# Even mixer's feature norms: sums of all heads as rows of one tile, one pass of roots, spread by split-format products, squares shared between two engines

## The reference, cut to what matters

```
def rms_norm(x, g):
    xf = x.astype(jnp.float32)
    y = xf * lax.rsqrt(jnp.mean(jnp.square(xf), axis=-1, keepdims=True) + EPS)
    return (y * g.astype(jnp.float32)).astype(x.dtype)

    qn = rms_norm(q, q_norm).reshape(B, S, G, R, dk)
    ks_blk = to_blocks(rms_norm(k_sel, k_norm[1]))
    kw_pad = jnp.pad(rms_norm(k_win, k_norm[2]), pad)
    q = (rms_norm(c_q, cq_norm) @ w_uq).reshape(B, S, H, dn + dr)
    kv = (rms_norm(c_kv, ckv_norm) @ w_ukv).reshape(B, S, H, dn + dv)
```

## Time and profile before

| | before |
|---|---|
| median of three runs | 2292.04 us |
| lowest and highest run | 2291.61, 2302.24 us |
| the profiled execution's own time | 2293.38 us |
| its span, first to last instruction | 2291.6 us |
| PE, DVE, ACT, POOL busy | 93%, 56%, 43%, 8% of the span |
| mean granted TensorE clock | 0.970 of 2.4 GHz |

### The profile page before, as it was taken

One profiled execution on the slowest core, in us unless ns is written; L12 is line 12 of the kernel. 1 busy time (PEld: TensorE's weight loads), 2 busy tenths in 40 slices (PEclk: granted clock), 3 DMA queues, 4 the chain that ended last, 5 costly groups with the idle time before them and its releaser, 6 DMA issues. The chain is left out here.

```text
span 2291.6 us, 33139 instructions
## 1 busy us (share of the span) xinstructions
PE 2137.0 (93%) x12537; PEld 1652.5 (72%) x12537; DVE 1284.4 (56%) x1814; ACT 994.1 (43%) x1308; POOL 186.9 (8%) x182
## 2 busy tenths in 40 slices
PE   7987898999999999998999999998999789988998
PEld 5764434788888878888887888786577368777776
DVE  3367756353233234434666666888367754525888
ACT  2146636252123121121656665774243643414774
POOL 0010000000000000000311101011112300002011
PEclk9999989999999999998999999999999899988999
DMA  8007001153144135012878877995220000126996
GB/s 251 12 10 250 37 16 40 37 152 101 61 119 124 33 98 178 1 37 96 278 272 277 287 267 271 385 391 217 78 74 28 12 1 1 75 84 199 389 373 258
DMA packets 220721, 336.42 MB, mean 147 GB/s; under 512 B 50413, under 2 KB 135309, under 8 KB 220606
## 3 DMA queue, kind: packets, MB, share of 16 engines
q1 hardware_dynamic: 213470, 314.53, 40.6%
q0 software_dynamic: 7136, 20.34, 2.5%
HBM read 306.82 MB, written 26.95 MB: 146 GB/s over the span
## 5 line engine op out<-in xcount | busy, mean ns | idle before, releaser
L1550 DVE TENSOR_TENSOR moe_pass_wL<-moe_pass_w,moe_pass_wH 128x2048 fp32r<-128x2048 f32 (+1 forms) x144 | 303.4, 2112 | 113.2 <-ACT moe_pass_wH L1474 113.1
L1474 ACT ACTIVATE moe_pass_wH<-moe_pass_w 128x2048 fp32r<-128x2048 f32 (+1 forms) x144 | 254.7, 1772 | 130.4 <-PE PS L568 90.9
L1550 DVE TENSOR_TENSOR hm_pass_wL<-hm_pass_w,hm_pass_wH 128x2048 fp32r<-128x2048 f32 x60 | 135.7, 2287 | 36.3 <-ACT hm_pass_wH L1474 36.3
L566 PE MATMUL PS<-moe_pass_wL,moe_pass_xgH 128*128 128x512 f32 (+1 forms) x384 | 147.3, 384 | 6.9 <-DVE moe_pass_wL L1550 4.5
L568 PE MATMUL PS<-moe_pass_wH,moe_pass_xgH 128*128 128x512 f32 (+1 forms) x384 | 142.7, 372 | 0.0
L567 PE MATMUL PS<-moe_pass_wH,moe_pass_xgL 128*128 128x512 f32 (+1 forms) x384 | 142.6, 371 | 0.0
L566 PE MATMUL PS<-xnT_low,ffn_upH 128*128 128x512 f32 x352 | 140.2, 398 | 0.3 <-PE PS L568 0.3
L568 PE MATMUL PS<-ffn_xH,ffn_upH 128*128 128x512 f32 x352 | 138.3, 393 | 0.0
L567 PE MATMUL PS<-ffn_xH,ffn_up_low 128*128 128x512 f32 x352 | 137.6, 391 | 0.0
L73 PE MATMUL PS<-ones,ident 128*128 128x128 f32 x926 | 120.9, 293 | 13.4 <-PEq L42 11.1
L73 PEld LDWEIGHTS PS<-ones,ident 128*128 128x128 f32 x926 | 116.9, 207 | 18.3 <-issue 15.4
(11 more groups left out here) (843 smaller groups left out, 4946.1 us busy)
## 6 DMA issues: line engine op xcount, KB each, us to landing
moe_pass_w<-in_moe_w_down SPq DMA_DIRECT2D x40, 1024.0 KB, 6.9
moe_pass_w<-in_moe_w_gate SPq DMA_DIRECT2D x32, 1024.0 KB, 7.0
moe_pass_w<-in_moe_w_up SPq DMA_DIRECT2D x32, 1024.0 KB, 7.8
hm_pass_w<-in_exp_w_gate SPq DMA_DIRECT2D x40, 512.0 KB, 6.9
hm_pass_w<-in_exp_w_up SPq DMA_DIRECT2D x40, 512.0 KB, 6.9
hm_pass_w<-in_exp_w_down SPq DMA_DIRECT2D x40, 512.0 KB, 6.6
od_W<-in_od_w_in SPq DMA_DIRECT2D x12, 1024.0 KB, 11.2
moe_pass_w<-in_moe_w_gate SPq DMA_DIRECT2D x16, 768.0 KB, 6.9
```

The source lines that it names most:

```text
L566: nc.tensor.matmul(out, lh, rl, start=start, stop=False)
L1474: nc.scalar.activation(wH[:, i % S, 0:n], w[:, i % R, 0:n], ACT.Copy).then_inc(s["high"], 1)
L1550: nc.vector.tensor_tensor(wL[:, i % S, 0:n], w[:, i % R, 0:n], f32(wH[:, i % S, 0:n]), ALU.subtract) \
```

## The change

Six things are changed, all in or for `ev_hidden`:

- **Squares.** ACT squares the tiles 0, 2, 4, 6, 8 and POOL the tiles 1, 3, 5, 7, into nine buffers that are not reused.
- **Sums.** PE multiplies each square by its own 128x46 slice of a constant (`norm_sums`), accumulating all nine in one PSUM bank. Row r of 14 holds head r's mean square (rows 0 to 11 the heads, 12 cq, 13 ckv); rows 32 to 45 hold the same again.
- **Roots.** Ln, Exp and the Newton step are made once, over 46x512.
- **Split.** DVE rounds the 46 rows to fp32r into `both` (which POOL has zeroed), and then overwrites rows 32 to 45 by the low part.
- **Spread.** PE multiplies `both` by a constant of zeros and ones (`norm_spread`, rounded once by DVE at the stage's start, at the address of pcT) and so puts each head's root on the partitions of its head, one fp32r product per group, in four PSUM banks. DVE's final multiplication reads the root from PSUM.
- **Order.** PE makes the sums first, then hidden 0 and 1, roots 0 to 3, hidden 2, roots 4 to 7, hidden 3, and 12 instead of 40 `stay_busy` products. Two loads (212 KB and 524 KB) are added in the middle of `smalls`.

```
+    srcs = [src for grp in groups for src in grp["src"]]
+    high, low = slice(0, FSUMS), slice(LOW, FSUMS)
+    by_act = range(0, len(srcs), 2)
...
             nc.gpsimd.memset(ec[:, :], EPS).then_inc(s["eps"], 1)
+            nc.gpsimd.memset(f32(both[:, :]), 0.0).then_inc(s["eps"], 1)
+            for m, src in enumerate(srcs):
+                if m not in by_act:
+                    nc.gpsimd.tensor_tensor(sq[:, m], src, src, ALU.mult).then_inc(s["squared_p"], 1)
...
-            def sums(g):
-                if g >= NB:
-                    pe.wait_ge(s["normed"], first[g - NB + 1])
-                for i, src in enumerate(groups[g]["src"]):
-                    m = first[g] + i
-                    pe.wait_ge(s["squared"], m + 2)
-                    nc.tensor.matmul(PS[:, g % NB, :], groups[g]["ones"], sq[:, m % 4], start=i == 0,
-                                     stop=i == len(groups[g]["src"]) - 1).then_inc(s["summed"], 1)
+            def sums():
+                pe.wait_ge(loaded["small"], small)
+                for m in range(len(srcs)):
+                    if m in by_act:
+                        pe.wait_ge(s["squared_a"], m // 2 + 1)
+                    else:
+                        pe.wait_ge(s["squared_p"], m // 2 + 1)
+                    ins = nc.tensor.matmul(PS[high, 0, :], row_sum[:, m], sq[:, m], start=m == 0, stop=m == len(srcs) - 1)
+                ins.then_inc(s["summed"], 1)
...
+            def roots(g):
+                pe.wait_ge(s["rstd"], 1)
+                pe.wait_ge(s["spread_high"], 1)
+                if g >= 4:
+                    pe.wait_ge(s["normed"], done[g - 3])
+                nc.tensor.matmul(root_bank(g), row_spread[:, g], both[:, :], start=True, stop=True).then_inc(s["roots"], 1)
...
-            stay_busy(nc, C, 40, 4)
+            stay_busy(nc, C, 12, 4)
...
+            for m in by_act:
+                nc.scalar.activation(sq[:, m], srcs[m], ACT.Square).then_inc(s["squared_a"], 1)
+            act.wait_ge(s["eps"], 1)
+            act.wait_ge(s["summed"], 1)
+            nc.scalar.activation(rs[:, :], PS[high, 0, :], ACT.Ln, bias=ec[high, 0:1]).then_inc(s["logged"], 1)
+            act.wait_ge(s["logged"], 1)
+            nc.scalar.activation(rs[:, :], rs[:, :], ACT.Exp, scale=-0.5).then_inc(s["rooted"], 1)
...
+            nc.vector.tensor_copy(row_spread[:, :, :].rearrange("p a b -> p (a b)"), row_whole[:, :, :].rearrange("p a b -> p (a b)"))                 .then_inc(s["spread_high"], 1)
...
+            y, t = rs[:, :], tt[:, :]
+            dve.wait_ge(s["rooted"], 1)
+            step(nc.vector.scalar_tensor_tensor(out=t, in0=PS[high, 0, :], scalar=EPS, in1=y, op0=ALU.add, op1=ALU.mult))
+            step(nc.vector.scalar_tensor_tensor(out=t, in0=t, scalar=-0.5, in1=y, op0=ALU.mult, op1=ALU.mult))
+            step(nc.vector.scalar_tensor_tensor(out=y, in0=t, scalar=1.5, in1=y, op0=ALU.add, op1=ALU.mult))
+            dve.wait_ge(s["eps"], 2)
+            step(nc.vector.tensor_copy(both[high], y))
+            nc.vector.tensor_tensor(both[low], rs[low], f32(both[low]), ALU.subtract).then_inc(s["rstd"], 1)
+            for g, grp in enumerate(groups):
+                dve.wait_ge(s["roots"], g + 1)
+                for src, gain, dst in zip(grp["src"], grp["gain"], grp["dst"]):
+                    nc.vector.scalar_tensor_tensor(out=dst, in0=src, scalar=gain, in1=root_bank(g),
+                                                   op0=ALU.mult, op1=ALU.mult).then_inc(s["normed"], 1)
```

More of the change, by code:

```diff
@@ L1706 @@
 NH, HD = 8, 64
+LOW, FSUMS = 32, 46
 CMP_L, CMP_S = 32, 16
@@ L1757, in head_of_row, with norm_rows, norm_sums, norm_spread @@
     return pick
+def norm_rows():
+    rows = np.zeros((P, 9, 14), np.float32)
+    for p in range(P):
+        for m in range(6):
+            rows[p, m, 2 * m + p // HD] = 1.0
+    rows[:, 6:8, 12] = 1.0
+    rows[:, 8, 13] = 1.0
+    return rows
+def norm_sums():
+    count = np.array([HD] * 12 + [2 * P, P], np.float32)
+    out = np.zeros((P, 9, FSUMS), np.float32)
+    for a in (0, LOW):
+        out[:, :, a:a + 14] = norm_rows() / count
+    return out.reshape(P, 9 * FSUMS)
+def norm_spread():
+    out = np.zeros((P, 8, P), np.float32)
+    for a in (0, LOW):
+        out[a:a + 14] = norm_rows()[:, (0, 1, 2, 3, 4, 5, 6, 8)].transpose(2, 1, 0)
+    return out.reshape(P, 8 * P)
 def gains_by_row(q, k):
@@ L2035, in mixer_even, with norms_and_hidden, root_bank @@
         nc.all_engine_barrier(sem_only=True)
-def norms_and_hidden(nc, C, groups, kc, vc, X, pos, pair, w1, hid, hid4, gate, gq, gm, flip, flip32, loaded, small, load_table):
-    B, NB = 4, 4
-    G = len(groups)
-    batches = [range(a, min(a + B, G)) for a in range(0, G, B)]
-    with ExitStack() as mem, stage(nc, "ev_hidden", "ready spread X_taken squared summed logged rstd steps normed hid_made gelu sigmoid copied made") as (block, s):
-        sq = mem.enter_context(nc.sbuf_tensor("ev_hidden_sq", [P, 4, SEQ], F32))
-        rs = mem.enter_context(nc.sbuf_tensor("ev_hidden_rs", [P, 2 * B, SEQ], F32))
-        tt = mem.enter_context(nc.sbuf_tensor("ev_hidden_tt", [P, 2, SEQ], F32))
+def norms_and_hidden(nc, C, groups, kc, vc, X, pos, pair, w1, hid, hid4, gate, gq, gm, flip, flip32, loaded, small, load_table, row_sum, row_whole, row_spread):
+    srcs = [src for grp in groups for src in grp["src"]]
+    high, low = slice(0, FSUMS), slice(LOW, FSUMS)
+    by_act = range(0, len(srcs), 2)
+    with ExitStack() as mem, stage(nc, "ev_hidden", "ready spread spread_high X_taken eps squared_a squared_p summed logged rstd steps roots rooted normed hid_made gelu sigmoid made") as (block, s):
+        sq = mem.enter_context(nc.sbuf_tensor("ev_hidden_sq", [P, len(srcs), SEQ], F32))
+        rs = mem.enter_context(nc.sbuf_tensor("ev_hidden_rs", [FSUMS, SEQ], F32))
+        tt = mem.enter_context(nc.sbuf_tensor("ev_hidden_tt", [FSUMS, SEQ], F32))
+        both = mem.enter_context(nc.sbuf_tensor("ev_hidden_both", [P, SEQ], F32R))
         ec = mem.enter_context(nc.sbuf_tensor("ev_hidden_eps", [P, 1], F32))
         PS = C.PS
-        first = [0]
-        for g in groups:
-            first.append(first[-1] + len(g["src"]))
         hids = [(v, a) for v in range(2) for a in range(2)]
+        done = [0]
+        for grp in groups:
+            done.append(done[-1] + len(grp["src"]))
+        def root_bank(g):
+            return PS[:, (g + 1) % 4, :]
         @block.sync
@@ L2061, in _ @@
         def _(pool):
[L2062 to L2069 removed]
+            nc.gpsimd.memset(ec[:, :], EPS).then_inc(s["eps"], 1)
+            nc.gpsimd.memset(f32(both[:, :]), 0.0).then_inc(s["eps"], 1)
+            for m, src in enumerate(srcs):
+                if m not in by_act:
+                    nc.gpsimd.tensor_tensor(sq[:, m], src, src, ALU.mult).then_inc(s["squared_p"], 1)
             step = Steps(pool, s["made"])
@@ L2108, in _ @@
                     spread(v, g)
-            for g in range(NB):
-                sums(g)
+            sums()
             pe.wait_ge(loaded["cmp"], 96)
             hidden(0)
-            for n, gs in enumerate(((4, 5), (6,), (7,)), 1):
-                for g in gs:
-                    sums(g)
-                hidden(n)
+            hidden(1)
+            for g in range(4):
+                roots(g)
+            hidden(2)
+            for g in range(4, len(groups)):
+                roots(g)
+            hidden(3)
             pe.wait_ge(s["gelu"], 1)
-            stay_busy(nc, C, 40, 4)
+            stay_busy(nc, C, 12, 4)
         @block.scalar
         def _(act):
-            act.wait_ge(s["squared"], 1)
-            for batch in batches:
-                for g in batch:
-                    act.wait_ge(s["summed"], first[g + 1])
-                    nc.scalar.activation(rs[:, g], PS[:, g % NB, :], ACT.Ln, bias=ec[:, 0:1], scale=1.0 / groups[g]["n"]).then_inc(s["logged"], 1)
-                for g in batch:
-                    act.wait_ge(s["logged"], g + 1)
-                    nc.scalar.activation(rs[:, g], rs[:, g], ACT.Exp, scale=-0.5).then_inc(s["rstd"], 1)
+            for m in by_act:
[5 more added lines that the diff above has]
+            nc.scalar.activation(rs[:, :], rs[:, :], ACT.Exp, scale=-0.5).then_inc(s["rooted"], 1)
             for n, (v, a) in enumerate(hids):
```

39 lines of the change are left out of this document (7 added, 32 removed).

## The result

| | before | after |
|---|---|---|
| median, runs of the same job | 2293.43 us (6) | 2275.44 us (6) |
| ratio, 95% interval | | 0.9905 [0.9887, 0.9924] |
| own time and span of the profiled execution | 2293.38, 2291.6 us | 2268.78, 2266.9 us |
| PE's first product of `ev_hidden` to its first of `ev_compressed` | 46.6 us | 31.7 us |
| mean granted clock | 0.970 | 0.975 |

By the ratio the kernel is 0.95% faster [0.76, 1.13]; the forecast was 0.64%. The time lies within the range of 2273 to 2284, without the long execution at its very edge.

A forecast was written before the change was run, and what follows sets the result against it. TensorE bounds the kernel, but ev_hidden is bound by waiting; PE's end there moves from 157.26 to 142.6, saving 14.6 us. From 2293.38 that gives 2278.8, less 1.3 for the median: 2277.4 us, range 2273 to 2284.

The forecast's parts named there:

- The 0.6 us that PE was to wait for the roots: In ev_hidden after hidden 0 and 1: PE free at 130.3, roots at 130.9, its only wait.
- Edits costed at nothing: Squares, spread-constant cast and two added loads of ev_hidden: all covered by other work, 0 us on the path.
- the up to 2 us that the cast and a POOL square were allowed to cost each other: Early ev_hidden: cast and POOL square may block each other, about 2 us at worst, within 7 us of cover.
- the idle time of 4.47 us and the half clock behind it: In ev_hidden from 122.68 us: PE's wait for DVE and the 1.2 GHz stretch 124 to 131, both to disappear.
- A shorter DVE chain alone nothing: End of ev_hidden: DVE ends at 155.54, PE at 157.26, so shortening DVE's chain alone gains nothing.
- a shorter tail of PE alone would bring 1.7 us: End of ev_hidden: fewer stay_busy products alone gain only PE's lead over DVE's last copy, 1.7 us.
- Two of the three runs agree within 0.5 us: Whole kernel before: this agreement was the argument against the rival of a varying clock, chance 0.19.
- The rival of the clock that gives part back: Later stages: low-clock stretches may not move with the program, losing 3 to 5 us, 2280.4 to 2282.4; chance 0.19.
- The sign of being wrong: Stages behind ev_hidden, same instructions: prediction wrong if they take more than 2 us longer in sum.
- 46 rows of output: Rival, ev_hidden: sums writing 46 rows let the clock fall, 5 to 10 us lost, 2282 to 2287; chance 0.04.
- the loss of 35 us: Rival, latent stage: low clock starts earlier, costing 35 us less the 14.6 gained, 2312; chance 0.02.
- The tail of 12 keeps PE warm: Against the rival that the shorter tail leaves PE cold in ev_compressed, 2 to 5 us, 2279 to 2282; chance 0.07.

The follow-up runs named there:

- pool_squares: The changed kernel with all nine squares on POOL instead of five of them on ACT; 2277.12 us, ratio 0.9932 to the kernel before.
- spread_rows128: The changed kernel with roots spread by plain fp32 products over 128 rows, 114 of them zero, without cast and split; 2283.23 us, ratio 0.9928 to before.
- before_filled: The kernel before with 19 stay_busy products where PE waited 4.47 us for the first normalised tile; 2291.56 us, ratio 0.9990.
- tail40: The changed kernel with 40 stay_busy products at the stage's end as before, instead of 12; 2289.57 us, ratio 0.9976 to the kernel before.
- after_again: The changed kernel run and profiled once more, no edit; 2279.06 us, ratio 0.9908 to the kernel before.
- whole_spread: The changed kernel with roots spread by plain fp32 products of the 14 rows alone, without cast and split; 2297.23 us, ratio 0.9999 to the kernel before.
- before_tail12: The kernel before with 12 stay_busy products instead of 40 at the stage's end, nothing else changed; 2295.64 us, ratio 0.9999.

## Why the prediction was wrong in a size and right in its mechanism

- **After the change: right to under 1 us.** The sums were forecast from 115.6 to 123.3 and ran from 116.14 to 124.1 (PE began 0.5 us later; 0.3 of it are two copies of the pair constant that take 0.67 us in place of 0.36, beside POOL's new memset). First Newton step 127.5 forecast, 128.10 measured; roots 130.9, 131.44; last norm ended 139.5, 139.86; PE's end 142.6, 143.40; cast 0.65, 0.68; tail 2.8, 2.90. The 0.6 us that PE was to wait for the roots shows in no idle time, but the two hidden products ahead of them last 7.45 us (123.99 to 131.44) where one lasts 3.49, so some 0.5 us of it are there.
- **Edits costed at nothing: right.** Cast, shared squares and two DMAs left no wait on the path. pool_squares shows that the sharing brings nothing either. Of the up to 2 us that the cast and a POOL square were allowed to cost each other, 0.5 came: the cast took 0.68 us and did not wait, the square that POOL began 0.03 us behind it took 1.55 us, the others 1.03 to 1.04. In spread_rows128, which has no such cast, all four squares take 1.03 to 1.04.
- **The step that failed is the size of "the idle time of 4.47 us and the half clock behind it".** It was taken from one profile, in which the half clock lasts 7 us. In three of five profiles it lasts 14, the second low stretch, in the tail, is longer too, and the stage takes 52.4 us. On the mean of the five the stage gives 18.3 us and not the 14.6 of the sum, so this term was taken 3.5 us too small. before_filled shows that the wait is the cause of the first low stretch. The sum itself, for the profile that it was read from, came out: 46.6 less 31.7 is 14.9.
- **"A shorter DVE chain alone nothing" was wrong.** tail40, all of the change but the tail, is the nearest case: the mean is 5.8 ± 1.7 us below before and the stage 38.0 us. The long tail waits for the fourth Gelu, and this comes earlier when the wait and the half clock ahead of it are gone. Of the other half, "a shorter tail of PE alone would bring 1.7 us", 0.4 ± 1.8 was measured: the stage did get shorter, and the next one took it back.
- **The evidence was there and was read wrongly.** "Two of the three runs agree within 0.5 us" was put against a varying clock; the third run was 10 us higher. The mean of 110 executions is 2296.0, not the 2292.04 on which the forecast stood. The base 4.0 too low and the gain 5.1 too low are why 2277.4 lies only 1.1 from the measured mean of 2276.3: two errors that cancel, which is luck. The forecast of the gain has no such luck: 0.64% forecast, 0.95% measured.
- **The rival of the clock that gives part back came true in two places and was outweighed in a third.** +1.8 and +2.3 us in the stretches behind the stage, where every profile of before has the same length to 0.1 us and each of after a longer one: my price of 3 to 5 us. Against it the last router at -6.3. The sign of being wrong, more than 2 us longer behind the stage in sum, did not come on the mean (4.9 us shorter), though one of the four profiles, after_again, is 4.6 us longer there than the profile that the forecast was read from. By the Trainium skill ("TensorE: Matmul & The Clock Gate", What's actually happening) the window of activity is free-running. That work moved in time therefore meets it elsewhere is my conclusion. The segments behind the stage, which hold the same instructions, agree in that they change length by -8 to +5 us; it does not tell why the five profiles of before, which reach them up to 7.9 us apart, have `ev_compressed` to `ev_latent_heads` at one length.
- **The other rivals.** 46 rows of output did not let the clock fall (1.00 through the stage); the latent stage did not become the loss of 35 us, it went from 53.6 to 55.9. The tail of 12 keeps PE warm and a tail of none does not.
- **What stays open.** The -6.3 of the last router: its short length is in 4 of 4 profiles after and in 1 of 5 before, in kernels where nothing near it differs, and what decides it was not found. It does not belong to the changed stage as such: pool_squares, with the same stage of 31.7 us, has 16.2 us there, spread_rows128 16.2 and whole_spread 17.3, while before_tail12 has 11.8. Nor is it the wait ahead of the router, which pool_squares and after_again both lack. The means of the table's seven differences sum to -23.7 us, while all executions say -19.7 ± 1.1, so the profiled ones overstate it. That the 3.7 us above the forecast in the stage (18.3 for 14.6) and the rest from elsewhere add up to the 5.1 is therefore within the error and not shown term by term.

## What to carry to other kernels

Before pricing the removal of a wait on PE, take several profiles of the kernel before: what stands behind the wait at half clock may have two lengths, and the runs' spread, here 10 us among three, already says so. Where two engines end a stage together, time the two edits apart and together: here they gave 5.8 and 0.4 us alone and 19.7 together. Give operands of few rows their full rows, with a second part of the value or with zeros, and look at what becomes of the time: it was worth 16 us for the roots here, and in the latent stage no gain on the mean is shown, since a wait opened behind it.

## What the runs showed of the hardware that was not expected

- **Operands of few rows let the clock fall while PE is never idle.** 14 rows of 128: low for 27 us, hidden products behind them 7.09 us instead of 3.68; the same products with 114 zero rows: 1.00. 8 rows in the latent stage: low for 17 to 24 us in every profile with them; with 120 zero rows that stretch is gone. Few rows of output (46, in the sums; 8, in the latent sums from 310.5) do not. Both cases are fp32 products, and no number of rows between 14 and 128 was tried in their place.
- **One wait, two prices.** The same 4.47 us wait was followed by 7 us at 1.2 GHz in some executions and by 14 in others, in the same kernel. In the profiles the short one came where PE reached the stage at 112.0 to 112.2 us, the long one where it did at 113.6 to 114.1; what links the two was not tested. Filled with products, the wait was followed by no low clock at all (1.00 from 112 to 143).
- **A product of fp32r of 512 columns** starts 0.26 us after the one before on the mean (four in 1.04, from 131.44 to 132.48 in the kernel after); one of fp32 with the same shape took 0.87 (four in 3.49, from 132.91 to 136.40 in spread_rows128).
